# Router logits taken from the sums ahead of the second norm, with 128-column products, low rows in VectorE's waits, and the norm's scales by column applied behind the masks

## The reference

```python
h = memory_cross_attention(x, mem, xattn_wq[l], xattn_wk[l], xattn_wv[l], xattn_wo[l])
x = layer_norm(ALPHA * x + h, ln2_g[l], ln2_b[l])     # (x - mu) * rsqrt(var + EPS) * g + b
h = grouped_moe(x, router_w, router_b, moe_w_gate[l], moe_w_up[l], moe_w_down[l])
x = layer_norm(ALPHA * x + h, ln3_g[l], ln3_b[l])
# grouped_moe: scores = sigmoid(x @ router_w); sel = scores + router_b; 16 experts in 4 groups;
# the best group by the sum of its two best sel, then the two best experts in it;
# gates = their scores, divided by their sum; out = sum over e of
# gates[:, e] * ((silu(x @ w_gate[e]) * (x @ w_up[e])) @ w_down[e])
```

## Time and profile before

| what | us |
|---|---|
| runs of the kernel | 731.64 to 732.11, median 732.1 |
| the profiled execution | 732.65 |
| its span on the core | 730.9 |
| PE busy in the span | 706.7 |
| DVE busy | 402.4 |
| ACT busy | 271.2 |
| POOL busy | 46.2 |

### The profile page before, as it was taken

The page is one execution under the profiler, slowest core; times in us unless marked ns, Lnnn a source line. Parts: engine busy times, 40 slices in busy tenths (PEclk is TensorE's granted clock), DMA queues, the critical chain, the costliest instruction groups (busy, mean ns, idle before and its releaser), DMA issues.

```text
span 730.9 us, 11978 instructions
## 1 busy us (share of the span) xinstructions
PE 706.7 (97%) x4792; PEld 568.8 (78%) x4792; DVE 402.4 (55%) x702; ACT 271.2 (37%) x465; POOL 46.2 (6%) x87
## 2 busy tenths in 40 slices
PE   8999999999999999999799999999999999999992
PEld 8979987889988875556499798888898897655651
DVE  5685885674457622121478588848646575212125
ACT  4555743455533131111424465434555131311121
POOL 1700000010002300000111000001000000000000
PEclk9999999999999999999989999999999999999997
DMA  8991344573357799999985313545733494999961
GB/s 280 331 368 66 108 142 173 182 233 117 115 179 298 249 387 389 415 418 412 342 276 171 119 59 116 173 170 176 231 116 116 176 397 194 353 422 415 418 273 60
DMA packets 62638, 176.09 MB, mean 241 GB/s; under 512 B 3840, under 2 KB 37040, under 8 KB 53360
## 3 DMA queue, kind: packets, MB, share of 16 engines
q1 hardware_dynamic: 58112, 161.69, 59.9%
q0 software_dynamic: 4032, 12.24, 5.1%
q10 hardware_dynamic: 432, 1.31, 0.5%
HBM read 174.18 MB, written 1.05 MB: 240 GB/s over the span
## 4 chain that ended last, share of the span: by engine, by line
PE 55%; issue 35%; DVE 5%; POOL 2%; DVEq 1%; ACT 0%; POOLq 0%; ACTq 0%
PE ring L1607 7%; PE ring L1609 7%; PE ring L1608 7%; PE quad L1607 7%; PE quad L1608 7%; PE quad L1609 6%; PE ring L1906 2%; PE ring L1873 2%; PE ring L1775 1%; PE ring L1668 1%; PE ring L1649 1%; PE ring L1678 1%; DVE X L1067 1%; PE ring L1685 1%; DVE w_lo L969 1%
## 5 line engine op out<-in xcount | busy, mean ns | idle before, releaser
L969 DVE TENSOR_TENSOR w_lo<-raw,w_hi 128x1024 fp32r<-128x1024 f32 x108 | 127.8, 1222 | 44.9 <-ACT w_hi L664 34.5
L664 ACT CAST w_hi<-raw 128x1024 fp32r<-128x1024 f32 x108 | 107.9, 1049 | 65.0 <-PE quad L1609 60.2
L1607 PE MATMUL ring<-x_hi,w_hi 128*128 128x256 f32 x320 | 93.5, 292 | 1.4 <-ACTq L707 0.7
L1608 PE MATMUL ring<-x_lo,w_hi 128*128 128x256 f32 x320 | 91.3, 285 | 0.0
L1609 PE MATMUL ring<-x_hi,w_lo 128*128 128x256 f32 x320 | 91.2, 285 | 0.0
L687 ACT ACTIVATE arena<-ring 128x512 f32<-128x512 f32 (+1 forms) x66 | 35.6, 573 | 85.6 <-PE ring L1609 66.3
L1607 PEld LDWEIGHTS ring<-x_hi,w_hi 128*128 128x128 f32 x320 | 62.1, 194 | 3.1 <-issue 1.9
L1608 PEld LDWEIGHTS ring<-x_lo,w_hi 128*128 128x128 f32 x320 | 62.0, 194 | 0.7 <-issue 0.5
L1525 DVE TENSOR_TENSOR y_lo<-ring,y_hi 128x512 fp32r<-128x512 f32 x32 | 22.1, 692 | 72.9 <-ACT y_hi L923 72.9
L1609 PEld LDWEIGHTS ring<-x_hi,w_lo 128*128 128x128 f32 x320 | 62.1, 194 | 0.0
L2042 PE MATMUL ring<-raw,x_slots 128*64 128x256 f32 x448 | 51.3, 380 | 0.0
(11 more groups left out here) (309 smaller groups left out, 1396.1 us busy)
## 6 DMA issues: line engine op xcount, KB each, us to landing
raw<-in_moe_w_gate SPq DMA_DIRECT2D x20, 1024.0 KB, 7.0
raw<-in_moe_w_up SPq DMA_DIRECT2D x16, 1024.0 KB, 7.8
w_raw<-in_moe_w_up SPq DMA_DIRECT2D x16, 1024.0 KB, 9.3
w_raw<-in_moe_w_down SPq DMA_DIRECT2D x16, 1024.0 KB, 11.1
raw<-in_w_in SPq DMA_DIRECT2D x14, 1024.0 KB, 11.4
raw<-in_moe_w_down SPq DMA_DIRECT2D x12, 1024.0 KB, 10.1
raw<-in_w_out SPq DMA_DIRECT2D x10, 1024.0 KB, 4.9
raw<-in_xattn_wk SPq DMA_DIRECT2D x8, 1024.0 KB, 6.5
```

Of the source, the lines that this page charges most:

```text
L664: nc.scalar.copy(unit_slot(u, 0, n)[:, s], raw[:, SLOT[u], s]).then_inc(hi_done, 1)
L969: low = nc.vector.tensor_tensor(unit_slot(u, 1, n)[:, s], raw[:, SLOT[u], s], unit_slot(u, 0, n)[:, s].bitcast(F32), ALU.subtract)
L1607: mm(out, a_hi, b_hi, start=first, stop=False)
L1608: mm(out, a_hi, b_lo, start=False, stop=False)
```

## The change

- `second_norm` becomes `second_sums`. VectorE adds, takes statistics and hands the sums themselves over for turning; it also makes minus the mean. It does not apply the norm there.
- GpSimd's `ln_power(1)` makes `shift` = minus mean times 1/deviation after each power.
- The router's weights are multiplied by the gain and by the bias, and summed over a partition's columns, on VectorE ahead of the sums (`rw_parts`, `rt[:, 3]`). TensorE sums these over all partitions with one more product, and multiplies the turned sums with `rw_row`, 128 columns wide where 16 are wanted. VectorE puts the logits together from these: product times 1/deviation, plus shift times the gain part, plus the bias part.
- ScalarE makes `z` = X / deviation + shift (`normal`) and takes the high rows from it; VectorE takes the low rows of tile 0 in two parts, one of them ahead of the last add of tile 1. All four turned parts are moved by ScalarE. One exp serves both tiles.
- Gain and bias of the second norm are loaded by column (`ln2_cols`) and applied where the gathered rows are moved out of PSUM. Loaded by row (`ln2_w`, into `y_hi` and `y_lo`) they are applied to X in `second_affine`, in the expert stage, for the third norm's sum.
- The filler products are 27 in one place instead of 4, 7, 3 and 26 in four.

The diff, cut to its core:

```diff
-    jobs += [("xc0", "act"), ("xc1", "act"), ("rt0", "act"), ("xc2", "act"), ("xc3", "dve"), ("rt1", "act")]
+    jobs += [(f"xc{i}", "act") for i in range(4)] + [("rt0", "dve"), ("rt1", "dve")]
...
                         nc.gpsimd.tensor_tensor(lr[:, t:t + 1], lv[:, t:t + 1], minus_half[:, 0:1],
                                                 ALU.pow).then_inc(ln_rstd, 1)
+                        if i == 1:
+                            pool.drain()
+                            nc.gpsimd.tensor_tensor(shift[:, t:t + 1], neg_mean[:, t:t + 1], lr[:, t:t + 1],
+                                                    ALU.mult).then_inc(shift_ready, 1)
...
+                if l == 0:
+                        pool.dma_start(ln2_cols[:, 0], ln2_g.rearrange("l (p c) -> p l c", c=DC)).then_inc(cols_full, 16)
+                        pool.dma_start(ln2_cols[:, 1], ln2_b.rearrange("l (p c) -> p l c", c=DC)).then_inc(cols_full, 16)
                 ln_power(0)
-                load_ln(ln2_g[l], ln2_b[l], 3 * l + 1)
+                load_ln(ln3_g[l], ln3_b[l], 2 * l + 1)
                 ln_power(1)
-                load_ln(ln3_g[l], ln3_b[l], 3 * l + 2)
+                pool.wait_ge(unit_used, used(U_O + 3, l))
+                pool.dma_start(ln2_w[0], ln2_g[l].partition_broadcast(P)).then_inc(ln2_full, 16)
+                pool.dma_start(ln2_w[1], ln2_b[l].partition_broadcast(P)).then_inc(ln2_full, 16)
...
-                turned_x(0)
-                turned_x(1)
-                act.wait_ge(unit_used, used(U_O + 3, l))
-                rows_high(0)
-                logits_exp(0)
-                turned_x(2)
-                rows_high(1)
-                logits_exp(1)
+                def normal(t):
+                    act.wait_ge(shift_ready, l * T + t + 1)
+                    nc.scalar.activation(z[:, t, :], X[:, t, :], ACT.Identity, bias=shift[:, t:t + 1], scale=lr[:, t:t + 1])
+                normal(0)
+                act.drain()
+                rows_high(0, slice(0, DC // 2))
+                rows_high(0, slice(DC // 2, DC))
+                for j in range(4):
+                    turned_x(j)
+                normal(1)
+                act.wait_ge(dve_emptied, emptied("rt1", l))
+                nc.scalar.activation(rt[:, 1], rt[:, 1], ACT.Exp, scale=-1.0).then_inc(scores_ready, 1)
+                act.drain()
+                rows_high(1, slice(0, DC))
...
+            def second_sums(l, done, count, rows_low):
                 dve.wait_ge(quad_ready, l * 3 + 2)
                 norm_added(0)
+                dve.sem_inc(x_ready, 1)
+                for a in range(2):
+                    norm_part(0, a)
+                norm_var(0, negated=True)
                 dve.wait_ge(half_ready, l + 1)
                 norm_add(1, 0)
                 dve.drain()
                 norm_part(1, 0)
+                rows_low(0, slice(0, DC // 2), 1)
                 dve.wait_ge(done, count)
                 norm_add(1, 1)
+                dve.drain().then_inc(x_ready, 1)
+                dve.sem_inc(quad_free, 1)
                 norm_part(1, 1)
+                norm_var(1, negated=True)
+                dve.wait_ge(shift_ready, l * T + T)
+            def second_affine(l):
+                dve.wait_ge(ln2_full, 32 * (l + 1))
+                for t in range(T):
+                    nc.vector.scalar_tensor_tensor(X[:, t, :], X[:, t, :], mv[:, t, 0:1], ln2_w[0], ALU.subtract, ALU.mult)
+                dve.drain()
+                for t in range(T):
+                    nc.vector.scalar_tensor_tensor(X[:, t, :], X[:, t, :], lr[:, t:t + 1], ln2_w[1], ALU.mult, ALU.add)
+                dve.drain().then_inc(dense_x, 1)
...
+                for a in range(2):
+                    nc.vector.tensor_tensor(rw_parts[:, a], rw[:], view(ln2_cols[:, a, l, :], [[1, DC], [0, E]]), ALU.mult)
+                dve.drain()
+                for a in range(2):
+                    nc.vector.tensor_reduce(rt[:, 3, a, :], rw_parts[:, a].rearrange("p c e -> p e c"), AX_X, ALU.add)
+                dve.drain().then_inc(router_ready, 1)
...
+                second_sums(l, unit_used, used(U_O + 3, l), rows_low)
+                rows_low(0, slice(DC // 2, DC), 2)
+                dve.wait_ge(misc_ready, misc_done("rt0", l))
+                nc.vector.tensor_copy(sel, bank("rt0")[:, P:P + 2 * E].rearrange("p (a e) -> p a e", a=2))
+                dve.drain()
+                for t in range(T):
+                    nc.vector.scalar_tensor_tensor(rt[:, 0, t, :], sel[:, 0, :], shift[:, t:t + 1], sel[:, 1, :],
+                                                   ALU.mult, ALU.add)
+                dve.drain()
+                for t in range(T):
+                    if t:
+                        dve.wait_ge(misc_ready, misc_done("rt1", l))
+                    nc.vector.scalar_tensor_tensor(score[:, t, :], bank(f"rt{t}")[:, 0:E], lr[:, t:t + 1], rt[:, 0, t, :],
+                                                   ALU.mult, ALU.add).then_inc(dve_emptied, 1)
+                dve.wait_ge(scores_ready, l + 1)
...
-                            nc.scalar.copy(late_rows(r)[:, c, :], gather_bank(1, c)).then_inc(gath_act, 1)
+                            nc.scalar.activation(late_rows(r)[:, c, :], gather_bank(1, c), ACT.Identity,
+                                                 bias=ln2_cols[:, 1, l, k:k + 1],
+                                                 scale=ln2_cols[:, 0, l, k:k + 1]).then_inc(gath_act, 1)
...
                     one_hot(1, 1)
+                    second_affine(l)
...
+                    if t == 0:
+                        mm(o[:, P:P + 2 * E], every, rt[:, 3].rearrange("p a e -> p (a e)"), start=True, stop=True)
                     for k in range(DC):
-                        r = mm(o[:, 0:E], xT[:, k, t * P:(t + 1) * P], rw[:, k, :], start=k == 0, stop=k == DC - 1)
+                        r = mm(o[:, 0:P], xT[:, k, t * P:(t + 1) * P], rw_row[:, E * k:E * k + P], start=k == 0, stop=k == DC - 1)
...
-                transpose_x("xc", l, 2, (0,))
-                keep_busy("xc2", l, 4)
-                pe.wait_ge(act_emptied, emptied("xc1", l))
-                logits(0)
-                keep_busy("xc2", l, 7)
-                transpose_x("xc", l, 2, (1,))
-                keep_busy("rt1", l, 3)
-                pe.wait_ge(act_emptied, emptied("xc2", l))
-                pe.wait_ge(dve_emptied, emptied("xc3", l))
-                logits(1)
-                keep_busy("gb1", l, 26)
+                transpose_x("xc", l, 2)
+                pe.wait_ge(router_ready, l + 1)
+                pe.wait_ge(act_emptied, emptied("xc1", l))
+                logits(0)
+                pe.wait_ge(act_emptied, emptied("xc3", l))
+                logits(1)
+                keep_busy("gb1", l, 27)
```

More of the change, by code:

```diff
@@ L301, in hybrid_trunk_kernel @@
         rt = at(5632, 7, T * E).rearrange("p a (t e) -> p a t e", t=T)
+        rw_parts = at(4352, 2, DC * E).rearrange("p a (c e) -> p a c e", c=DC)
+        rw_row = at(4352, 2 * DC * E)
         precede = at(4352, 8, PER_GROUP * PER_GROUP)
         precede2 = at(4480, 8, PER_GROUP * PER_GROUP)
-        xn_hi = rounded("xn_hi", 0, T, DC, P)
-        xn_lo = rounded("xn_lo", 2048, T, DC, P)
+        xn_hi = rounded("xn_hi", 2048, T, DC, P)
+        xn_lo = rounded("xn_lo", 0, T, DC, P)
+        z = at(6144, T, D)
+        ln2_w = [nc.alloc_sbuf_tensor_at(f"ln2_w{i}", [P, D], F32, offset=Y_HI + 4 * YC * SEQ * i)[:] for i in range(2)]
         s_t = at(4096, 2, FF)
@@ L634, in _ @@
                                         channel_multiplier=1).then_inc(ws_masked, 1)
+                if l == 0:
+                    with nc.allow_non_contiguous_dma(reason="a norm's gain and bias by column"):
+                        pool.dma_start(ln2_cols[:, 0], ln2_g.rearrange("l (p c) -> p l c", c=DC)).then_inc(cols_full, 16)
+                        pool.dma_start(ln2_cols[:, 1], ln2_b.rearrange("l (p c) -> p l c", c=DC)).then_inc(cols_full, 16)
                 ln_power(0)
-                load_ln(ln2_g[l], ln2_b[l], 3 * l + 1)
+                load_ln(ln3_g[l], ln3_b[l], 2 * l + 1)
                 ln_power(1)
-                load_ln(ln3_g[l], ln3_b[l], 3 * l + 2)
+                pool.wait_ge(unit_used, used(U_O + 3, l))
+                pool.dma_start(ln2_w[0], ln2_g[l].partition_broadcast(P)).then_inc(ln2_full, 16)
+                pool.dma_start(ln2_w[1], ln2_b[l].partition_broadcast(P)).then_inc(ln2_full, 16)
                 if l + 1 < DEPTH:
@@ L902, in early_move @@
                             act.wait_ge(gathered, l * 16 + (c + 1))
-                            nc.scalar.copy(x_slots[:, :, c, :],
-                                           gather_bank(0, c).rearrange("p (a b) -> p a b", a=2)).then_inc(gath_act, 1)
+                            nc.scalar.activation(x_slots[:, :, c, :], gather_bank(0, c).rearrange("p (a b) -> p a b", a=2),
+                                                 ACT.Identity, bias=ln2_cols[:, 1, l, c:c + 1],
```

(23 more changed lines are left out.)

77 lines of the change are left out of this document (42 added, 35 removed).

## The result

| | before | after |
|---|---|---|
| median of the runs, us | 732.09 (731.64 to 732.11, 4 runs) | 723.27 (723.08 to 723.39, 4 runs) |
| profiled execution, us | 732.65 | 723.37 |
| its span, us | 730.9 | 721.6 |
| ratio | | 0.9876, 95% interval 0.9863 to 0.9888 |

The kernel is 8.8 us faster; 725.7 was forecast, and the range began at 724.1. The profiled executions are 9.3 us apart, since that of before lay 0.56 above its median and that of after 0.10.

A forecast was written before the change was run, and what follows sets the result against it. TensorE's chain from VectorE's last add through norm, transposes, logits and its own filler was taken to set the experts' start. 3.39 - 0.2 = 3.2 us a layer, 6.4 in two: 732.1 - 6.4 = 725.7, range 724.1 to 728.8.

The forecast's parts named there:

- the path to the logits: Router stage: statistics, power and norm passes leave TensorE's path to the counts; gain 3.39 us a layer.
- tile 0's lateness: Second norm, tile 0: shift, high and low rows may delay the last add; 0.2 us a layer, bounds 0 and 0.5.
- what was costed at nothing: Ranking behind tile 1's logits and work off the path, such as `second_affine`, hidden by cover or idle time; cost 0.
- The four passes: `second_affine` on VectorE in the expert stage: slot gates about 0.8 us late, taken up by 2.4 of margin.
- the sum: Whole kernel: 3.39 - 0.2 = 3.2 us a layer, 6.4 in two, giving 725.7.
- The low end, 724.1: Bottom of the range, allowing the half-clock stretch between layers to begin or end up to a microsecond of work differently.
- GpSimd is late: Rival, chance 0.22: long gaps before GpSimd's power delay ranking or last add, 1 to 2.5 us; say 727.3.
- Table loads: Rival, chance 0.04: ScalarE's `normal` needs another table than exp, 2.57 us a layer; 730.8.
- The gain is lost in the expert stage: Rival, chance 0.05: DMAs, not weight slots, set the expert stage's pace, so its end stays; 732.1.
- The wide products cost what the page's gap says: Rival, chance 0.03: 128-column router products on TensorE cost 1.0 us a layer more; 727.7.
- TensorE's clock falls: Rival, chance 0.06: a wait in the new stage lowers the clock, 0.113 more per logits or filler record; up to 735.4.
- the products are as wide as the filler: Argument against the clock's fall in the router stage, beside TensorE's remaining waits of about 0.1 us.

The follow-up runs named there:

- power0: The changed kernel with GpSimd's power for tile 0 of the second norm made twice, with a drain between; 723.97 us, ratio 0.9887 to the kernel before.
- filler22: The changed kernel with 22 filler products instead of 27 behind the logits; 722.77 us, ratio 0.9874 to the kernel before.
- power1: The changed kernel with GpSimd's power for tile 1 of the second norm made twice; 722.72 us, a single time.
- affine6: The changed kernel with two more VectorE passes behind the four of `second_affine`, written where nobody reads; 726.12 us.
- pad192: The kernel before with an unread buffer putting `arena` 192 bytes further, nothing else changed; 730.81 us, ratio 0.9983 to the kernel before.
- oldbase: The changed kernel with its three new small buffers behind `arena`, so `arena` keeps its old address; 724.09 us, ratio 0.989 to the kernel before.
- pad32: The kernel before with `arena` 32 bytes further; 732.41 us, a single time.
- pad64: The kernel before with `arena` 64 bytes further; 731.73 us, a single time.
- narrow: The changed kernel with router products of 16 columns instead of 128; 726.36 us.

## Why the prediction was right in part, and where it was wrong

**Right: the stage.** By its own steps, the path to the logits was forecast as last add, plus 1.78 to the end of the transposes, plus 3.82 for extra product and logits, plus 6.10 of filler: 11.70. It took 11.60. The extra product cost 0.14 and not 0.2. The gain forecast from these steps was 3.39; measured 3.49 and 3.51.

**Mis-sized: tile 0's lateness.** I took 0.2 a layer between bounds of 0 and 0.5. It was 0. Counted back from the last add, which itself came 0.64 earlier, shift was ready 3.75 ahead of it (223.52 to 227.27), where 3.7 to 3.3 was forecast: the negated mean added only 0.07 to VectorE's step, GpSimd's gap was 0.34 instead of 0.48, and the multiply took 0.19, its lower bound. The operations behind it were longer than I had (two half casts in 2.35, a low half in 1.20) and ended just in time. power0 shows that the mechanism is there, with 0.1 of margin. This term is 0.4 us in two layers.

**Right in kind: what was costed at nothing.** The ranking started at 233.57 (against the last add 6.3 behind; forecast 6.3), and ended 0.26 ahead of the counts; filler22 and power1 confirm that the two engines are nearly level and what covers them. The four passes made the slot gates 1.0 late (255.20, behind TensorE's last row of theirs at 253.94 + 0.25; forecast 0.8), and the two moves by less than their margin; that margin is 1.0, not the 1.6 that 2.4 - 0.8 gives (affine6). `normal` took 1.245, at the upper of its two bounds, and a scaled move 0.777 instead of 0.6, 0.18 more. SP still waits for TensorE in the expert stage:

```profile
SPq L508 <- PE ring L2121: 57.3, 14, 19.4
SPq L508 <- PE ring L2156: 24.0, 5, 5.0
```

81.3 us where it was 86.6, and the stage keeps the gain (-4.13 in, -4.06 out; -8.98 in, -8.99 out).

**The step that failed: the sum.** "3.39 - 0.2 = 3.2 a layer, 6.4 in two" took the router stage for the whole of the change. Nothing outside was priced, above all not the allocation, though the kernel has three new tensors ahead of `arena`: that term was put at nothing without a reason, and it measured 1.2 us. Of the 2.4 us that I missed, by medians:

- 0.6 in the stage itself (7.0 instead of 6.4);
- 1.2 from the address: four units a layer at 0.15 each, shown by pad192 and oldbase from both sides;
- 0.3 at the third norms, 0.17 in each layer: GpSimd's gap between the plain operation and the power is 1.62 where it was 1.80, and 0.32 where it was 0.48, and VectorE's passes behind it start 0.17 earlier. All nine kernels that have the change show the short gaps, and all five that don't, the padded ones and before, the long ones. Why the gap is shorter was not tested;
- 0.2 to 0.3 remain. Two executions of one kernel differ by as much. The stretch ahead of the query products of layer 0 may hold some of it: it took 166.3 to 166.7 in the nine traces with the change and 166.7 to 167.8 in the five without, though 166.74 in both profiled executions compared above.

```profile
359.54 1.08 POOL L637 TENSOR_TENSOR lr<-lv,minus_half 128x1 f32<-128x1 f32 x2 [1.62 <-issue]
...
711.66 1.16 POOL L637 TENSOR_TENSOR lr<-lv,minus_half 128x1 f32<-128x1 f32 x2 [0.32 <-issue]
```

The other 0.14 of the 0.3 behind the last scatter lies between the issue of the output's DMA and the end of the span, a stretch that varies from 3.9 to 4.6 among the runs.

Of the 0.77 between the layers only that 0.17 is a gain of the change. All kernels that were run, the padded ones of before too, show 0.56 to 0.79 less there than the profiled execution of before (pad32 0.61, pad64 0.62, pad192 0.60). That execution lost some 0.6 there, about as much as it lies over its median (0.56). TensorE's clock had been low there for longer, 0.62 in 361.00 to 367.00 against this in after (all five engines), four us earlier like the work:

```profile
357.00:363.00 6.00, 2.94 (x13) 2.65 (x13) 4.20 (x6) 2.27 (x5) 2.75 (x5) 0.72 0.86 252
```

The low end, 724.1, allowed a microsecond for just this stretch; the gain came from elsewhere. With `arena` at its old address the change measures 724.09 (oldbase), at that low end and still 1.6 below the forecast: the address is the largest term that was missed, not the only one.

**The rivals.** *GpSimd is late* did not come: its gaps were 0.34 and 0.17, and in layer 1 0.17 for tile 1. power0 and power1 price it: 0.6 a layer for 0.7 us at tile 0, nothing at tile 1. I had charged tile 1 with 0.8 to 1.1 for 1.3; its cover is at least 0.6, so 1.3 would cost 0.7 at most. *Table loads*: none. *The gain is lost in the expert stage*: no. *The wide products cost what the page's gap says*: 0.114 against 0.112 in narrow, 0.06 a layer instead of 1.0. The Trainium skill (TensorE: Matmul & The Clock Gate, "Back-to-back issue gap") gives its 25 to 56 ns for the isolated gap of one product, and says that in a stream of weight loads and products the spacing is set by both. The records here are such a stream, so the prediction had applied the wrong figure of that section; the two measured steps agree with its sentence on streams in that the width alone doesn't set them.

*TensorE's clock falls* did not come either, but I had put it on a wait, and had dismissed it since "the products are as wide as the filler". narrow shows that this clause carried the weight. With 16 columns the clock falls without any wait, and half of the stage's gain is lost. The change has two parts that need each other: products gathered into one row of 32, and their width. I had costed the width as a price (0.002 a record) and never asked what it buys.

## What to carry to other kernels

Read a diff's allocations as edits: every buffer behind a new tensor moves, and its readers' steps may change, here by 2% of a unit. Rows of the same form in a stage that the change doesn't touch show it at once, when marks are compared from the start and not from the changed stage. And ask of every odd size in a diff what it buys, not only what it costs.

## What the runs showed that I had not expected

- The place of `arena` in SBUF, which holds operands, changes the step of fp32r products of 256 columns, without any change in form: 7.48 us for the third or fourth unit at the old place, and 7.425, 7.39, 7.405, 7.33 and 7.405 at 32, 64, 128, 192 and 384 bytes further. The rule is open.
- TensorE can be busy by its records without a gap and yet be granted less than its full clock: 0.80 to 0.92 in windows of 6 us around and behind 34 records of 32 and 16 columns, 1.00 with 128 columns in place of the 16.
- A record of 16 columns behind a weight load of 128 steps nearly as long as one of 128 (0.112 and 0.114 us).
- GpSimd's gap between two small operations with a drain between them is 0.15 to 0.34 us in the second norm. Between the plain operation and the power of the third norms it is 1.62 and 0.32 in after, where the same two lines of code had 1.80 and 0.48 before; at the first norm of layer 0 it is 2.21 where it was 2.04. A multiply of 128x1 takes 0.19, a power 0.54 to 0.56.
